# Placing the last two experts' rows for three of five tiles, and gathering the stored rows for the other two

## The chip, the cores and the metric

The kernel runs on one core of a Trainium2 chip. The metric is the device time of one execution in microseconds (us); the time of a kernel is the median over its runs. One further execution was recorded by the hardware profiler: its span is the time from the first to the last instruction. Engines: PE (TensorE) multiplies matrices, DVE (VectorE) and ACT (ScalarE) work on tiles of 128 partitions, POOL (GpSimd) issues the indirect DMAs, SP (SyncE) issues most other DMAs.

## What is computed

One layer of a diffusion trunk with a linear-attention mixer, then a mixture of experts. 640 tokens (128 of context, 512 latent) pass through. The end of it is what matters here: each token takes the weighted outputs of two of 16 gated experts, adds them to its residual row, and the sum is normalised.

```python
# hier_moe: combine holds the two weights of each token's two picks
up = jnp.einsum('td,edf->tef', hf, p['moe_w1'])
gate = jnp.einsum('td,edf->tef', hf, p['moe_w3'])
act = jax.nn.silu(gate) * up * combine[:, :, None]
return jnp.einsum('tef,efd->td', act, p['moe_w2']).reshape(B, T, D)
...
x = x + (ga2 * hier_moe(h2, p)).astype(x.dtype)
...
y_prompt = rmsnorm(x, final_g)
```

## The kernel before

The 640 tokens are five tiles (NT = 5) of 128 rows by 1024 columns; tile 0 is the context. Each engine has its own instruction list, and the lists meet in semaphores; the order of each list is the order in which its code is written. PSUM is eight banks that a list of jobs (`jobs`) takes in turn.

**Experts.** Experts run in rounds; round r serves the slots r*128 to r*128 + 127 of every expert, and later rounds are entered only if some expert has more than 128 tokens. In a round, POOL gathers the tokens of each expert's 128 slots (`gather_rows`, L941), PE turns them, multiplies by the up and gate weights (job "ug"), DVE and ACT form the gated activations (L2002 to L2007; ACT's exponential and copies, all at L966), PE turns those (job "aT") and multiplies by the down weights (jobs "dn", two halves of 512 columns). DVE multiplies each half by a gain (weight times gate) on the way out of PSUM into `yo`, which has one buffer for even and one for odd experts (`rows_of`, L1995). The gain itself is made in two steps: ACT scales one row (`gain_b`), DVE adds the other part (L1990).

**How rows come back to tokens.** For experts 0 to 13 (LE = 14) ACT stores `yo` in DRAM (`rows_out`, L1310, tensor `expert_rows_dram`), 512 KB an expert. When these stores have landed, POOL issues ten indirect DMAs, two a tile: the first adds the row of each token's first pick into the residual `x1[:, t]` (L955), the second puts the row of the second pick in `second_rows[t]` (L958). A pick of expert 14 or 15 finds a row of zeros, written near the start (L679). Rows of experts 14 and 15 are never stored: PE places them, multiplying a 0/1 matrix (`own_slot`) by `yo`, two products for each half of each tile (jobs "sel").

**The end.** After expert 15's rows, DVE does for each tile: add `second_rows[t]` (L2020), add the two PSUM halves of the placed rows (L2024), and, one tile behind, the final scaling by the root of the mean square and the final gain (`final_rows`, L1954) into `acc`. ACT makes the root in between (a squaring pass with sum, a logarithm, an exponential), and SP stores each finished tile (L798).

Of the kernel before, what the change touches and what calls it, by code (L numbers as in the profile page):

```python
# [5 lines left out]
def trunk_program(nc, x_prompt, x_sample, state_rwkv, state_gla, c, c_ctx, norm1_g, norm2_g, w_ada, b_ada,  # L6
# [37 lines left out]
    LE = NE - 2  # L44
    CH = 64
# [13 lines left out]
    with ctx:  # L59
# [225 lines left out]
        ys_dram = nc.dram_tensor("expert_rows_dram", (NE * P, D), f32, kind="Internal").ap()  # L285
# [95 lines left out]
        for r in range(NT):  # L381
# [14 lines left out]
            jobs += [("sel", r, t, h) for t in range(NT) for h in range(2)]  # L396
# [187 lines left out]
        s_finr = sem("final_rstd")  # L584
        s_yout = sem("y_out")
# [66 lines left out]
        def _(sp):  # L652
# [15 lines left out]
            for i in range(RING, NS1):  # L668
# [4 lines left out]
                if i == 3 * RING:  # L673
# [15 lines left out]
            def inverse_back(h):  # L689
# [3 lines left out]
                if h == 0:  # L693
                    sp.wait_ge(s_zd, 48)
# [88 lines left out]
            def load_experts(r, count_known):  # L783
# [12 lines left out]
                for t in range(NT):  # L796
                    sp.wait_ge(s_yout, r * NT + t + 1)
                    sp.dma_start(y_prompt[0] if t == 0 else y_sample[0, (t - 1) * P:t * P, :], acc[:, t]).then_inc(s_ydma, 16)  # L798
# [6 lines left out]
        def _(pool):  # L805
# [127 lines left out]
            def gather_rows(r, count_known):  # L933
# [28 lines left out]
        def _(act):  # L962
# [42 lines left out]
            act.wait_ge(s_zd, 48)  # L1005
# [300 lines left out]
            def expert_copies(r, count_known):  # L1306
# [5 lines left out]
                act.wait_ge(s_ga2, 16)  # L1312
                for e in range(NE):
                    i = r * NE + e
                    if e == 0:
# [11 lines left out]
                    if i >= 2:  # L1327
                        act.wait_ge(s_yrow, i - 1)
                    if e == 0:
                        wait_result(act, "sw", r)  # L1330
                    tell(A(gain_b[e % 2], ga2b[:, 1], scale=slot_w[:, e:e + 1]), s_gain)
# [4 lines left out]
                for t in range(NT):  # L1336
                    wait_result(act, "sel", r, t, 1)
                    if r >= 1:
                        act.wait_ge(s_yout, (r - 1) * NT + t + 1)
# [7 lines left out]
        def _(dve):  # L1347
# [599 lines left out]
            def final_rows(r, t):  # L1947

                dve.wait_ge(s_finr, r * NT + t + 1)
                if r == 0 and t == 0:  # L1950
                    dve.wait_ge(s_fg, 16)
# [4 lines left out]
            def expert_gates(r, count_known):  # L1956
# [18 lines left out]
                own(STT(R["ib"], R["ps"], float(-(r + LE) * P), R["in"], ALU.add, ALU.mult))  # L1975
                own(TS(R["ib"], R["ib"], float(LE * P), None, ALU.add))
# [7 lines left out]

                def rows_of(e):
                    i = r * NE + e
                    at = r * (LE // 2) + e // 2
                    gain = gain_b[e % 2]
                    dve.wait_ge(s_gain, i + 1)
                    own(STT(gain, ga2b[:, 0], slot_w[:, NE + e:NE + e + 1], gain, ALU.mult, ALU.add))  # L1990
# [23 lines left out]
                rows_of(NE - 1)  # L2014
                if r == 0:
                    count_known()

                def rows_complete(t):
                    dve.wait_ge(s_yg[t], 32 * (r + 1))
                    own(TT(x1[:, t], x1[:, t], second_rows[t], ALU.add))  # L2020
# [12 lines left out]
        def _(pe):  # L2033
# [665 lines left out]
            def expert_products(r, count_known):  # L2699
# [57 lines left out]
                for t in range(NT):  # L2757
# [37 lines left out]
```

## Time and profile before

| | us |
|---|---|
| median of 3 runs | 942.36 |
| the three runs | 940.07, 942.71, 942.36 |
| the profiled execution | 939.88 |
| its span | 937.0 |

The profiled execution lies below the median of the runs; durations and waits are read from it. Over the whole span PE is busy 849.1 us (91%), DVE 566.8, ACT 331.2, POOL 155.2. The clock granted to PE is full in the stretch of the change until its last product; the mean over the span is 0.973. A line of the timeline gives start and duration in us, engine, source line, operation, output and inputs, shape, how often it stands in a row, and in brackets how long the engine was idle before it and what ended that. POOL's DMA lines show the time POOL spends to issue; "DMA to landing" is from the start of the issue to the last byte.

### The profile page before, as it was taken

The numbers are of one execution on the slowest core, as the hardware profiler recorded it, in microseconds if no ns is written. First come the engines' busy times: TensorE is split into PE (matmuls) and PEld (weight loads), VectorE is DVE, ScalarE is ACT, GpSimd is POOL, SyncE is SP. The second block draws the span as 40 slices with busy tenths as digits, with TensorE's granted clock in tenths as the row PEclk, the third lists the DMA queues.
The fourth block names the chain that finished last, engine by engine and source line by source line (L and its number), as shares of the span: only waits on it lengthen the run. The fifth ranks groups of instructions, "written<-read, shape, count | busy, mean of one in ns | idle before, by whom it ended". The sixth has DMA issues, their size and how long they took to land.

```text
span 937.0 us, 21506 instructions
## 1 busy us (share of the span) xinstructions
PE 849.1 (91%) x8890; PEld 518.2 (55%) x8890; DVE 566.8 (60%) x942; ACT 331.2 (35%) x582; POOL 155.2 (17%) x301
## 2 busy tenths in 40 slices
PE   2899999999999988988888888899994999999995
PEld 0455455566455454677777777745563544444542
DVE  2424036789988789666555565688356344444467
ACT  3221111142034467375667664312211222222213
POOL 7000111112000103424232231010002000000051
PEclk9999999999999999999999999999995999999998
DMA  9911323222255201111212222591064899999956
GB/s 332 382 39 65 130 91 101 91 84 80 86 179 180 91 0 27 36 24 32 44 33 37 42 43 54 186 351 77 26 222 132 287 358 370 362 365 372 311 142 220
DMA packets 120815, 142.44 MB, mean 152 GB/s; under 512 B 49996, under 2 KB 86280, under 8 KB 120328
## 3 DMA queue, kind: packets, MB, share of 16 engines
q1 hardware_dynamic: 111880, 116.55, 37.9%
q0 software_dynamic: 3744, 13.63, 4.7%
q10 hardware_dynamic: 5088, 10.82, 3.0%
q8 instruction: 73, 1.20, 0.5%
q14 instruction: 30, 0.25, 0.1%
HBM read 122.99 MB, written 18.00 MB: 150 GB/s over the span
## 4 chain that ended last, share of the span: by engine, by line
PE 79%; DVE 9%; DMA 4%; issue 3%; ACT 3%; SPq 0%; ACTq 0%; DVEq 0%; POOLq 0%
PE bank L2035 72%; PE bank L2039 7%; DMA region<-in_w_ada_dram 3%; DVE rk_r L1449 1%; ACT region L966 1%; DMA region<-in_w_in_dram 1%; DVE region L1449 1%; ACT ada_row_buffers L966 1%; DVE rk_r L1450 1%; DVE cl_b L1954 1%; DVE region L2024 1%; DMA rk_r<-h_rows_dram,slot_tokens 0%; DVE region L2020 0%; ACT w_sb L966 0%; DVE region L2003 0%
## 5 line engine op out<-in xcount | busy, mean ns | idle before, releaser
L2035 PE MATMUL bank<-region 64*64 64x64 f32 (+3 forms) x3900 | 399.2, 297 | 15.7 <-issue 6.1
L2035 PEld LDWEIGHTS bank<-region 64*64 64x64 f32 (+1 forms) x3900 | 231.2, 147 | 169.9 <-issue 158.8
L966 ACT ACTIVATE region<-bank 128x256 f32<-128x256 f32 (+3 forms) x215 | 97.2, 452 | 345.6 <-PE bank L2035 259.1
L2035 PE MATMUL bank<-region,rk_r 128*128 128x512 f32 x176 | 79.9, 608 | 0.8 <-issue 0.8
L2039 PE MATMUL bank<-ident,region 128*128 128x128 f32 (+2 forms) x403 | 61.7, 282 | 12.8 <-DMA region<-in_c_dram 10.9
L2039 PEld LDWEIGHTS bank<-ident,region 128*128 128x128 f32 (+2 forms) x403 | 44.1, 142 | 30.9 <-issue 23.5
L2002 DVE TENSOR_SCALAR region<-region 128x256 f32<-128x256 f32 x16 | 4.7, 295 | 93.3 <-ACT region L966 93.3
L1449 DVE SCALAR_TENSOR_TENSOR rk_r<-region,vec,rk_r 128x512 f32<-128x512 f32 x64 | 50.1, 783 | 11.1 <-ACT rk_r L966 9.0
L2035 PEld LDWEIGHTS bank<-region,rk_r 128*128 128x128 f32 x176 | 33.5, 196 | 39.5 <-issue 38.3
L941 POOL DMA_INDIRECT rk_r<-h_rows_dram,slot_tokens x16 | 16.0, 999 | 225.6 <-PE bank L2039 127.2
L1631 DVE TENSOR_TENSOR region<-bank,region 128x256 f32<-128x256 f32 x60 | 25.5, 424 | 39.2 <-PE bank L2035 37.9
L2035 PE MATMUL bank<-scratch,region 64*64 64x64 f32 (+1 forms) x688 | 41.7, 228 | 6.1 <-issue 3.2
L2035 PE MATMUL bank<-vtok_b,region 64*64 64x64 f32 x928 | 44.4, 222 | 1.6 <-DVE region L1660 1.6
L2035 PE MATMUL bank<-region,scratch 64*64 64x128 f32 (+1 forms) x512 | 35.8, 410 | 9.6 <-DMA region<-in_w_ada_dram 8.8
L2035 PEld LDWEIGHTS bank<-scratch,region 64*64 64x64 f32 (+1 forms) x688 | 39.1, 140 | 7.2 <-issue 7.2
L2035 PEld LDWEIGHTS bank<-vtok_b,region 64*64 64x64 f32 x928 | 41.3, 138 | 2.8 <-DVE region L1631 1.7
L966 ACT ACTIVATE region<-region 128x256 f32<-128x256 f32 (+1 forms) x27 | 24.7, 915 | 43.5 <-DVE region L1466 42.8
L966 ACT ACTIVATE ada_row_buffers<-bank 128x512 f32<-128x512 f32 x29 | 17.3, 597 | 55.0 <-PE bank L2039 51.0
L2035 PE MATMUL bank<-cl_b,ada_row_buffers 128*128 128x512 f32 x80 | 35.8, 596 | 0.1
L2035 PE MATMUL bank<-rk_r,ada_row_buffers 128*128 128x512 f32 x80 | 35.6, 593 | 0.0
L2035 PE MATMUL bank<-cl_b,rk_r 128*128 128x512 f32 x80 | 35.2, 593 | 0.0
L873 POOL TENSOR_TENSOR region<-kk_b,region 128x512 f32<-128x512 f32 x10 | 13.0, 1300 | 133.4 <-PE bank L2039 105.7
(283 smaller groups left out, 1137.2 us busy)
## 6 DMA issues: line engine op xcount, KB each, us to landing
region<-in_moe_w_dram SPq DMA_DIRECT2D x38, 1024.0 KB, 10.0
region<-in_w_ada_dram SPq DMA_DIRECT2D x12, 2048.0 KB, 8.8
region<-in_w_in_dram SPq DMA_DIRECT2D x6, 2048.0 KB, 9.1
cl_b<-in_moe_w_dram SPq DMA_DIRECT2D x10, 1024.0 KB, 11.1
expert_rows_dram<-yg_b ACTq DMA_DIRECT2D x14, 512.0 KB, 6.8
region<-late_condition_dram SPq DMA_DIRECT2D x3, 1024.0 KB, 9.4
a_rows_dram<-region SPq DMA_DIRECT2D x20, 128.0 KB, 2.5
region<-inverse_rows_dram SPq DMA_DIRECT2D x20, 128.0 KB, 3.0
```

The lines of the kernel that those rows point to most:

```text
L873: tell(pool.tensor_tensor(g.b, kkT[:, :, tok], aa[:, d, :, tok], ALU.mult), s_t1)
L941: pool.indirect_dma_start(out=xg[:, i % 3], out_offset=None, in_=h2_dram, in_offset=bass.IndirectOffsetOnAxis(ap=idx[:, e:e + 1], axis=0)) ...
L966: return act.activation(out, in_, func, **kw)
L1449: own(STT(out, lat[:, i:i + GH, j:j + GW], tap(c_, i, j), out, ALU.mult, ALU.add))
L1450: own(STT(dst[:, 0:P], line[:, 1:P + 1], tap(c_, 1, 1), dst[:, 0:P], ALU.mult, ALU.add))
L1631: out_of(TT(dst[:, hp::2], bank((n, h, hp))[:, 0:RC * HD].rearrange("p (h i) -> p h i", h=RC), src[:, hp::2], ALU.add), n, h, hp)
L1954: tell(STT(acc[:, t], x1[:, t], rstd[:, t:t + 1], fg, ALU.mult, ALU.mult), s_yout)
L2002: own(TS(sg[:, s], sg[:, s], 1.0, None, ALU.add))
L2024: out_of(TT(v, v, bank(("sel", r, t, h))[:, :], ALU.add), "sel", r, t, h)
L2035: return pe.matmul(out, lhsT, rhs, start=start, stop=stop)
L2039: return pe.transpose(out, in_, ident[0:n, 0:n])
```

## The change

PE places the last two experts' rows for tiles 0, 1 and 2 only (`PLACED = 3`). ACT stores the rows of experts 14 and 15 as well, and POOL waits for all sixteen stores before it gathers for tiles 3 and 4, whose picks of experts 14 and 15 now point at the stored rows. In the placed tiles such picks point at one added row of zeros (row NE*P), for which DVE makes one more small step and SP one more store near the start. The gain steps of experts 14 and 15 are moved ahead of expert 15's gate arithmetic on ACT and DVE. At the end DVE's list is rewritten: tile 0's add of gathered rows stands before expert 15's multiplies, those of tiles 1 and 2 before the placed rows are added, and the tiles are finished in the order 0, 1, 3, 2, 4 (`ROWS_ORDER`), on ACT and SP too.

```diff
+    PLACED = 3
+    ROWS_ORDER = (0, 1, 3, 2, 4)
...
-        ys_dram = nc.dram_tensor("expert_rows_dram", (NE * P, D), f32, kind="Internal").ap()
+        ys_dram = nc.dram_tensor("expert_rows_dram", (NE * P + 1, D), f32, kind="Internal").ap()
...
-            jobs += [("sel", r, t, h) for t in range(NT) for h in range(2)]
+            jobs += [("sel", r, t, h) for t in range(PLACED) for h in range(2)]
...
+                    sp.dma_start(ys_dram[NE * P:NE * P + 1, :].rearrange("a (b n) -> (a b) n", n=512), cl_b[0:2, 0:512]).then_inc(s_zd, 16)
...
                 for q in range(2):
-                    pool.wait_ge(s_ys[q], 16 * (r + 1) * (LE // 2))
-                pool.wait_ge(s_zd, 48)
+                    pool.wait_ge(s_ys[q], 16 * (r * (NE // 2) + LE // 2))
+                pool.wait_ge(s_zd, 64)
...
                 for t in range(NT):
+                    if t == PLACED:
+                        for q in range(2):
+                            pool.wait_ge(s_ys[q], 16 * (r + 1) * (NE // 2))
...
                 for e in range(NE):
                     i = r * NE + e
+                    if e == NE - 1:
+                        slot_gain(e)
...
-                    if 0 < e <= LE:
+                    if e < NE - 1:
+                        slot_gain(e)
+                    if e > 0:
                         rows_out(e - 1)
+                rows_out(NE - 1)
...
-                own(STT(R["ib"], R["ps"], float(-(r + LE) * P), R["in"], ALU.add, ALU.mult))
-                own(TS(R["ib"], R["ib"], float(LE * P), None, ALU.add))
+                own(STT(R["ib"], R["ps"], float(-(r + NE) * P), R["in"], ALU.add, ALU.mult))
+                placed = by_pick(R["ib"])[:, :, 0:PLACED]
+                own(STT(placed, placed, float((LE - NE) * P), placed, ALU.is_lt, ALU.mult))
+                own(TS(R["ib"], R["ib"], float(NE * P), None, ALU.add))
...
+                    if e == NE - 1:
+                        gain_of(LE)
+                        gain_of(NE - 1)
...
-                rows_complete(0)
-                for t in range(1, NT):
-                    rows_complete(t)
-                    final_rows(r, t - 1)
-                final_rows(r, NT - 1)
+                gathered(0)
+                rows_of(NE - 1)
+                if r == 0:
+                    count_known()
+                gathered(1)
+                gathered(2)
+                placed_rows(0)
+                placed_rows(1)
+                final_rows(r, 0)
+                gathered(3)
+                final_rows(r, 1)
+                placed_rows(2)
+                gathered(4)
+                final_rows(r, 3)
+                final_rows(r, 2)
+                final_rows(r, 4)
```

How the lists of DVE and POOL change in order. On DVE, from expert 15's gates to the end of the first two tiles, before (`yg_b` is `yo`, `region0` holds `second_rows`, `region3` is `x1`, `cl_b` is `acc`, L1990 the gain, L1995 the multiply):

```order
L2007 TENSOR_TENSOR region1<-bank4,region1 128x256
L1990 SCALAR_TENSOR_TENSOR region1<-region1,scratch 128x1024
L1995 TENSOR_TENSOR yg_b<-bank5,region1 128x512
L1995 TENSOR_TENSOR yg_b<-bank6,region1 128x512
L1996 MEMSET small 128x1
L1990 SCALAR_TENSOR_TENSOR kk_b<-region1,scratch,kk_b 128x1024
L1995 TENSOR_TENSOR yg_b<-bank0,kk_b 128x512
L1995 TENSOR_TENSOR yg_b<-bank1,kk_b 128x512
L1996 MEMSET small 128x1
L2020 TENSOR_TENSOR region3<-region3,region0 128x1024
L2024 TENSOR_TENSOR region3<-region3,bank2 128x512
```

And now (L2009 the gain, L2021 the multiply, L2045 the add of gathered rows, L2052 the add of placed rows):

```order
L2036 TENSOR_TENSOR region1<-bank4,region1 128x256
L2021 TENSOR_TENSOR yg_b<-bank5,region1 128x512
L2021 TENSOR_TENSOR yg_b<-bank6,region1 128x512
L2022 MEMSET small 128x1
L2045 TENSOR_TENSOR region3<-region3,region0 128x1024
L2021 TENSOR_TENSOR yg_b<-bank0,kk_b 128x512
L2021 TENSOR_TENSOR yg_b<-bank1,kk_b 128x512
L2022 MEMSET small 128x1
L2045 TENSOR_TENSOR region3<-region3,region0 128x1024 x2
L2052 TENSOR_TENSOR region3<-region3,bank2 128x512
```

The two gain steps are gone from behind the gates, and the adds of gathered rows of tiles 0, 1 and 2 stand ahead of the first placed rows.

On POOL, the gathers of expert rows of tiles 2, 3 and 4, before:

```order
L955 DMA region<-expert_rows_dram,pick_slots 128x1024
L958 DMA region<-expert_rows_dram,pick_slots 128x1024
L955 DMA region<-expert_rows_dram,pick_slots 128x1024
L958 DMA region<-expert_rows_dram,pick_slots 128x1024
L955 DMA region<-expert_rows_dram,pick_slots 128x1024 [waits filled]
```

And now:

```order
L962 DMA region<-expert_rows_dram,pick_slots 128x1024
L965 DMA region<-expert_rows_dram,pick_slots 128x1024
L962 DMA region<-expert_rows_dram,pick_slots 128x1024 [waits expert_rows_stored1,expert_rows_stored0]
L965 DMA region<-expert_rows_dram,pick_slots 128x1024
L962 DMA region<-expert_rows_dram,pick_slots 128x1024 [waits filled]
```

The order is the same; the seventh gather, tile 3's first, has a wait for the stores of both kinds of experts.

## Rows read from the trace of the kernel before

**Rows 1.** Timeline of PE: down products of expert 15, then all placing products.

```profile
905.41 3.70 PE L2035 MATMUL bank<-region 128*128 128x512 f32 x8 [0.53 <-ACT region L966]
909.58 17.41 PE L2035 MATMUL bank<-yg_b,vtok_b 128*128 128x512 f32 x40 [0.47 <-DVE yg_b L1995]
```

**Rows 2.** Timeline of DVE from expert 14's gain step to the last scaling.

```profile
904.42 1.28 DVE L1990 SCALAR_TENSOR_TENSOR region<-region,scratch 128x1024 f32<-128x1024 f32 x1
...
908.64 1.42 DVE L1995 TENSOR_TENSOR yg_b<-bank,kk_b 128x512 f32<-128x512 f32 x2
...
911.14 1.23 DVE L2020 TENSOR_TENSOR region<-region 128x1024 f32<-128x1024 f32 x1 [0.96 <-DVE small L1996]
...
916.79 0.69 DVE L2024 TENSOR_TENSOR region<-region,bank 128x512 f32<-128x512 f32 x1 [0.77 <-PE bank L2035]
...
918.84 1.23 DVE L2020 TENSOR_TENSOR region<-region 128x1024 f32<-128x1024 f32 x1
920.10 1.41 DVE L2024 TENSOR_TENSOR region<-region,bank 128x512 f32<-128x512 f32 x2
921.54 1.28 DVE L1954 SCALAR_TENSOR_TENSOR cl_b<-region,small,kk_b 128x1024 f32<-128x1024 f32 x1
922.86 1.23 DVE L2020 TENSOR_TENSOR region<-region 128x1024 f32<-128x1024 f32 x1
...
931.46 1.28 DVE L1954 SCALAR_TENSOR_TENSOR cl_b<-region,small,kk_b 128x1024 f32<-128x1024 f32 x1 [0.58 <-ACT small L966]
```

**Rows 3.** Timeline of POOL: gathers of expert rows (tiles 0, 0, 1, 2, 4).

```profile
899.40 1.57 POOL L955 DMA_INDIRECT region<-expert_rows_dram,pick_slots  x1 [42.03 <-DMA expert_rows_dram<-yg_b]
901.28 0.98 POOL L958 DMA_INDIRECT region<-expert_rows_dram,pick_slots  x1 [0.30 <-issue]
...
904.41 0.98 POOL L958 DMA_INDIRECT region<-expert_rows_dram,pick_slots  x1 [0.31 <-issue]
...
907.55 1.91 POOL L958 DMA_INDIRECT region<-expert_rows_dram,pick_slots  x1 [0.30 <-issue]
...
915.37 0.97 POOL L958 DMA_INDIRECT region<-expert_rows_dram,pick_slots  x1 [0.30 <-issue]
```

**Rows 4.** Line L958, one gather at a time: landing, tiles 0, 1, 2, 4.

```profile
DMA to landing us min/median/max: 6.4/6.4/6.4
...
DMA to landing us min/median/max: 7.4/7.4/7.4
...
DMA to landing us min/median/max: 8.1/8.1/8.1
...
DMA to landing us min/median/max: 8.2/8.2/8.2
```

**Rows 5.** DMA queues from 902 to 916 us: packets, MB, share of 16 engines.

```profile
q0 software_dynamic: 931, 3.42, 101.5%
```

**Rows 6.** Waits from 895 us to the end: total, times, longest us.

```profile
DVE region L2002 <- ACT region L966: 5.5, 1, 5.5
```

**Rows 7.** Busy time by stage (PE, PEld, DVE, ACT, POOL, PEclk, DMA share, GB/s).

```profile
897.00:898.00 1.00, 1.00 (x4) 0.41 (x3) 0.00 (x0) 0.00 (x0) 0.00 (x0) 1.00 0.99 406
```

**Rows 8.** Single stores: expert 13's rows, expert 12's, first output, last output.

```profile
L1310 ACTq DMA_DIRECT2D expert_rows_dram<-yg_b x1: 326/326/326, 896.0 to 896.0; - x1
DMA to landing us min/median/max: 2.6/2.6/2.6
...
DMA to landing us min/median/max: 4.7/4.7/4.7
...
DMA to landing us min/median/max: 5.6/5.6/5.6
...
DMA to landing us min/median/max: 3.8/3.8/3.8
```

**Rows 9.** Timeline of DVE: expert 0's gates, after the pick slots.

```profile
730.95 0.29 DVE L2002 TENSOR_SCALAR region<-region 128x256 f32<-128x256 f32 x1 [8.57 <-ACT region L966]
```

**Rows 10.** The page's DMA issues: KB each, median us to landing.

```profile
region<-in_moe_w_dram SPq DMA_DIRECT2D x38, 1024.0 KB, 10.0
...
region<-late_condition_dram SPq DMA_DIRECT2D x3, 1024.0 KB, 9.4
```

More of the change, by code:

```diff
@@ L584, in trunk_program @@
         s_finr = sem("final_rstd")
+        s_late = sem("late_tile_rows_complete")
         s_yout = sem("y_out")
@@ L693, in inverse_back @@
                 if h == 0:
-                    sp.wait_ge(s_zd, 48)
+                    sp.wait_ge(s_zd, 64)
                 if p >= 1:
@@ L795, in load_experts @@
                     count_known()
-                for t in range(NT):
-                    sp.wait_ge(s_yout, r * NT + t + 1)
+                for n, t in enumerate(ROWS_ORDER):
+                    sp.wait_ge(s_yout, r * NT + n + 1)
                     sp.dma_start(y_prompt[0] if t == 0 else y_sample[0, (t - 1) * P:t * P, :], acc[:, t]).then_inc(s_ydma, 16)
@@ L1312, in expert_copies, with slot_gain @@
                 act.wait_ge(s_ga2, 16)
+                def slot_gain(e):
+                    i = r * NE + e
+                    if i >= 2:
+                        act.wait_ge(s_yrow, i - 1)
+                    if e == 0:
+                        wait_result(act, "sw", r)
+                    tell(A(gain_b[e % 2], ga2b[:, 1], scale=slot_w[:, e:e + 1]), s_gain)
                 for e in range(NE):
                     i = r * NE + e
+                    if e == NE - 1:
+                        slot_gain(e)
                     if e == 0:
@@ L1326, in expert_copies @@
                     copy_out(aT[:, i % 2], ("aT", i), bank(("aT", i))[:, 0:FT * P].rearrange("p (f t) -> p f t", f=FT))
[L1327 to L1331, printed above, removed]
-                    if 0 < e <= LE:
+                    if e < NE - 1:
+                        slot_gain(e)
+                    if e > 0:
                         rows_out(e - 1)
+                rows_out(NE - 1)
                 if r == 0:
                     count_known()
-                for t in range(NT):
-                    wait_result(act, "sel", r, t, 1)
+                for n, t in enumerate(ROWS_ORDER):
+                    if t < PLACED:
+                        wait_result(act, "sel", r, t, 1)
+                    else:
+                        act.wait_ge(s_late, r * (NT - PLACED) + t - PLACED + 1)
                     if r >= 1:
-                        act.wait_ge(s_yout, (r - 1) * NT + t + 1)
+                        act.wait_ge(s_yout, (r - 1) * NT + n + 1)
                     own(A(junk, x1[:, t], ACT.Square, accum_out=rstd[:, t:t + 1]))
@@ L1947, in final_rows @@
             def final_rows(r, t):
-                dve.wait_ge(s_finr, r * NT + t + 1)
-                if r == 0 and t == 0:
+                n = ROWS_ORDER.index(t)
+                dve.wait_ge(s_finr, r * NT + n + 1)
+                if r == 0 and n == 0:
                     dve.wait_ge(s_fg, 16)
@@ L1983, in expert_gates, with gain_of @@
                     own(ins) if e < NE - 1 else tell(ins, s_own)
+                def gain_of(e):
+                    gain = gain_b[e % 2]
+                    dve.wait_ge(s_gain, r * NE + e + 1)
+                    own(STT(gain, ga2b[:, 0], slot_w[:, NE + e:NE + e + 1], gain, ALU.mult, ALU.add))
                 def rows_of(e):
                     i = r * NE + e
-                    at = r * (LE // 2) + e // 2
+                    at = r * (NE // 2) + e // 2
                     gain = gain_b[e % 2]
-                    dve.wait_ge(s_gain, i + 1)
-                    own(STT(gain, ga2b[:, 0], slot_w[:, NE + e:NE + e + 1], gain, ALU.mult, ALU.add))
+                    if e < LE:
+                        gain_of(e)
                     if at:
@@ L2012, in expert_gates, with gathered, placed_rows @@
                         rows_of(e - 1)
[L2014 to L2018, printed above, removed]
+                def gathered(t):
                     dve.wait_ge(s_yg[t], 32 * (r + 1))
-                    own(TT(x1[:, t], x1[:, t], second_rows[t], ALU.add))
+                    ins = TT(x1[:, t], x1[:, t], second_rows[t], ALU.add)
+                    own(ins) if t < PLACED else tell(ins, s_late)
+                def placed_rows(t):
                     for h in range(2):
@@ L2756, in expert_products @@
                 pe.wait_ge(s_own, r + 1)
-                for t in range(NT):
+                for t in range(PLACED):
                     for h in range(2):
```

2 lines of the change are left out of this document (1 added, 1 removed).

## The prediction

> **What bounds the kernel now.** The change touches only the last 37 us, so the question is what binds there, and the page's shares, which PE leads, can't tell. I read the timelines of PE and DVE for that stretch. PE finishes the down products of expert 15 and starts the placing products at 909.58; all forty of them take 17.41 us, 3.48 us a tile [rows 1]. DVE waits for PE only twice among the tiles, the second time at 916.79 for 0.77 us; from there it is never idle until the last tile, where it waits 0.58 us for ACT's root [rows 2]. A tile costs DVE 1.26 us for the add of the gathered rows (918.84 to 920.10), 1.44 for the two adds out of PSUM (to 921.54) and 1.32 for the final scaling: 4.02 us against PE's 3.48. The tail is DVE's. The last scaling starts at 931.46.
>
> The third view is POOL's timeline with the landing times. The ten gathers are issued from 899.40 to 915.37 and hold nothing up, because DVE asks for them late: those of tile 0 are in at 901.28 + 6.4 = 907.7, those of tile 2 at 907.55 + 8.1 = 915.65, those of tile 4 at 915.37 + 8.2 = 923.6, while the adds that use the first and the last begin at 911.14 and, two tiles after 918.84, at 926.9 [rows 2 to 4]. They are slow and they fill the DMA engines: from 902 to 916 the software queue moved 3.42 MB and took 101.5% of all sixteen [rows 5], 0.245 MB a us. So there is some slack between gather and use, 3.3 us at tile 4, and none in the DMA engines.
>
> **What is removed.** Sixteen of the forty placing products: 7.0 us of PE after 920 by 17.41/40 each, worth nothing to the end, since DVE was behind PE there. Four DVE adds out of PSUM, 2 x 1.44 = 2.9 us [rows 2]: these were on the path. The gain step of expert 15 (1.28 us, as long as a final scaling [rows 2]) moves ahead of the gate arithmetic, into the time in which DVE and ACT wait for the up product (DVE was idle 5.5 us there [rows 6]); the gain of expert 14 goes with it. Both were on the path between the gates and the placing products.
>
> **What takes their place on DVE.** Before, after expert 15's gates, gain, multiply, gain, multiply ran from 904.42 to 910.06 [rows 2]. Now the first multiply runs from 904.42 to 905.9. Then comes tile 0's add of gathered rows, ahead of expert 15's multiply, and its rows land at 907.7. It ends at 907.7 + 1.26 = 908.96. Expert 15's two multiplies are 0.72 each: 909.68 and 910.40, PE having its products ready by 909.1 (905.41 + 3.70 [rows 1]). So the gain step's 1.3 us are eaten by this wait, and expert 15's rows are ready 0.3 us later than before (908.64 + 1.42 [rows 2]). With the marker and the issue (0.15 us in before) ACT stores them at about **910.6**. Next is tile 1's add (landed 911.8 in before, perhaps 913 now), then tile 2's.
>
> Tile 2's rows: in before they landed at 915.65. By then 3.42 MB and the little before 902 had moved, of which 3.15 MB are tiles 0 to 2; the rest, some 0.4 MB or 1.6 us at 0.245 MB a us, was tile 3's and is gone from this place. Two stores of 0.52 MB come in, 1.3 us each at the 0.406 MB a us of the store of expert 13, which had the engines alone [rows 7]. Together 915.65 - 1.6 + 2.6 = 916.7. From the end of tile 2's add, 917.9, DVE has 2 x 1.44 + 1.32 = 4.2 us of work (tiles 0 and 1 placed, tile 0 scaled), then what is left needs tile 3's gathers: free at **922.1**.
>
> **The wait that is added.** POOL may issue tile 3's and tile 4's gathers only when the store of expert 15's rows has landed. Behind that wait stand four gathers on POOL; behind them stand DVE's adds of tiles 3 and 4, ACT's roots and the last three scalings. The price is the landing of a store issued at 910.6 into full DMA engines. The rows bound it: 2.6 us for expert 13's, alone; 4.7 for expert 12's, with weight loads going on; 5.6 for the first output, issued at 918.8 with tile 4's gathers in flight [rows 8]. The last is the nearest, since here too about six microseconds of gathers are queued, and I take it: 916.2. POOL started 0.8 us after the landing in before (896.0 + 2.6 = 898.6 to 899.40 [rows 3, 8]), so **917.0**.
>
> From there I copy the pattern of tiles 0 and 1, the other pairs that started into idle engines: issue 899.40, landed at +8.3 (907.7) and +12.4 (904.41 + 7.4 = 911.8) [rows 3, 4]. Tile 3's rows are in at **925.3** and tile 4's at **929.4**.
>
> DVE: tile 3's add 925.3 to 926.56, tile 1's scaling to 927.9, tile 2 placed to 929.3, tile 4's add from 929.4 to 930.66, scalings of tiles 3 and 2 to 933.3. ACT's root takes 1.28 + 0.58 = 1.9 us from the end of an add (in before the last scaling waited for it 0.58 us after the one ahead, which had begun when the add ended [rows 2]): 932.6 for tile 4, hidden. The last scaling starts at 933.3 against 931.46: **1.8 us later**. Its store goes out over the same idle engines (3.8 us then [rows 8]); it follows the one before it by 1.3 us, one transfer, so nothing is added.
>
> **Small terms.** One more DVE step on 128x6 in the pick slots, at most as much as a full scaling on 1024 columns did (1.28), with 8.57 us of idle time behind it [rows 9]: nothing. One 4 KB store and a count of 64 for 48 near 39 us, waited for much later: nothing. Picks of experts 14 and 15 in the placed tiles now all read one zero row instead of many. The nearest rows for reads of one address are the broadcast loads: 9.4 us for 1 MB against 10.0 for weights of the same size [rows 10]. So no loss is booked, and a gain is not either.
>
> The sum: 939.88 (profiled execution: span 937.0 and 2.88 around it) + 1.8 = 941.7. That execution lies 2.5 below the median of the three runs, 942.36, so against the median it is 942.36 + 1.8 = **944.2**.
>
> **A rule against the rows.** The second gathers of tiles 0, 1, 2 and 4 landed 6.4 to 8.2 us after their issue [rows 4], and a pair took about 4 us (907.7, 911.8, 915.65). "DMA: Bandwidth & Descriptors" of the Trainium skill (Anatomy of one DMA) gives a transfer from GpSimd about 2.0 us plus its bytes by 436 GB/s, which is an estimate of 3.2 us for half a megabyte. Tile 0's, into nearly idle engines, already took twice that. What it would make of the end is the third rival.
>
> **Rivals.** They all hang on when tile 4's gathers land. The end is unchanged when tile 4's add starts at 931.46 - 1.26 - 2 x 1.32 = 927.6, that is with POOL at 915.2 and the store landed 3.8 us after its issue.
> (1) The store gets through quickly, 2.6 us: POOL at 914.0, tile 3 in at 922.3, tile 4 at 926.4. DVE then binds: 922.3 and 1.26, 1.32, 1.44 make 926.3, and 926.4 and 1.26, 1.32, 1.32 make 930.3 for the last scaling, 1.2 us early: 941.2. For it: stores alone do that. Against: the engines are full at 910.6.
> (2) Slower: the gathers hold the store back until they are through (7 us or more: landed 917.6, POOL 918.4), and the outputs of tiles 0 and 1, 1.3 us of the engines each, now lie among tile 4's gathers. Tile 4 in at 930.8 to 932.1, the end 3.2 to 4.6 us late: 945.6 to 947.0. It counts as slower from a landing of 6.6 us on. For it: the 5.6 us row already reached past the end of tile 4's gathers (924.4 against 923.6). Against: weights and stores shared the engines in 4.7.
> (3) The gathers land in about 3.8 us, as a lone output store does; the engines' fullness would be a matter of how their time is counted. POOL at 914.0, tile 3 in at 919.7, tile 4 at 922.8, DVE binds throughout, from placed tile 1 (PE, 916.8) on: the last scaling near 927.6, 3.9 us early: 938.5. The Trainium skill's formula leads here. The landings of [rows 4] speak against it.
> That the change leaves work where it was is excluded: DVE's and PE's instruction lists show the steps gone.
>
> **Chances.** Forecast, 0.3 to 2.8 us later: 0.50. (1), 1.2 us early to 0.3 late: 0.22. (2): 0.22. (3): 0.06. A measurement here tells about 0.3%, 2.8 us, from no change. So faster 0.06, same 0.72, slower 0.22. The range leaves out (3) and the far end of (2) with the scatter of a median (0.07 to 2.3 us between the runs shown): 940.6 to 947.0. The likeliest case's own is 942.7 to 945.2.
>
> **What would show it.** In the profile of the changed kernel: DVE waits before the first add of gathered rows, to about 907.7; the last store of expert rows is issued near 910.6 and lands in 5 to 6 us; POOL has one gap of 6 to 7 us before the seventh gather, which starts near 917; PE ends 10 us after its first placing product; DVE waits for a DMA three times (tiles 2, 3 and briefly 4), and its last three scalings stand close together. If POOL starts again before 915.2, or DVE does not wait at tile 4, the forecast is wrong toward (1); if the gap of POOL ends after 918, toward (2). If tile 3's rows take much under 8.3 us from that start, my copy of the first pairs' pattern is the step that failed.

## The result and the profile after

The changed kernel takes 947.72 us (median of 14 runs, 941.51 to 952.73), the kernel before 941.35 (14 runs, 939.45 to 946.63). The ratio is 1.0063, with a 95% interval of 1.0042 to 1.0083: slower, by 5.9 us of 941. The forecast was 1.8 us slower, 944.2 us, called no change because 1.8 us is less than the 2.8 us that a measurement can tell; its range went up to 947.0.

The profiled execution took 950.49 us, its span is 948.7. Part of its distance to the kernel before is scatter between executions: expert 15's exponential on ACT, before which the two kernels do the same work, starts at 907.49 instead of 900.90. So I measure from that exponential in every trace ("after" is the changed kernel). To the end of the span it is 937.0 - 900.90 = 36.1 us in before and 948.7 - 907.49 = **41.2** in after, and the last scaling starts after 30.6 and 36.0 us. These 5.1 and 5.4 us are near the 5.9 of the runs, but the two are not the same quantity. The part of the device time that lies outside the span is 2.88 us in the profiled execution of before and only 1.8 in the changed kernel (1.70 to 1.84 in all 14 runs), so the span grew by about 1.1 us more than the time did. When both kernels ran again, the medians rose by 5.3 us in time and by 6.3 in span, and the stretch from the exponential by 6.2. What shortens the part outside the span is open; it also reads about 1.8 us in every other variant below but gain_moved and plain_gathers.

The timeline of DVE in after, from expert 14's multiply to the end (columns as in [rows 2]):

```profile
911.01 1.42 DVE L2021 TENSOR_TENSOR yg_b<-bank,region 128x512 f32<-128x512 f32 x2
...
914.47 1.23 DVE L2045 TENSOR_TENSOR region<-region 128x1024 f32<-128x1024 f32 x1 [1.92 <-DMA region<-expert_rows_dram,pick_slots]
915.73 1.42 DVE L2021 TENSOR_TENSOR yg_b<-bank,kk_b 128x512 f32<-128x512 f32 x2
...
919.79 1.23 DVE L2045 TENSOR_TENSOR region<-region 128x1024 f32<-128x1024 f32 x1 [2.52 <-DMA region<-expert_rows_dram,pick_slots]
925.04 1.28 DVE L2045 TENSOR_TENSOR region<-region 128x1024 f32<-128x1024 f32 x1 [4.02 <-DMA region<-expert_rows_dram,pick_slots]
926.36 2.85 DVE L2052 TENSOR_TENSOR region<-region,bank 128x512 f32<-128x512 f32 x4
929.60 1.28 DVE L1973 SCALAR_TENSOR_TENSOR cl_b<-region,small,kk_b 128x1024 f32<-128x1024 f32 x1 [0.39 <-ACT small L973]
934.14 1.22 DVE L2045 TENSOR_TENSOR region<-region 128x1024 f32<-128x1024 f32 x1 [3.25 <-DMA region<-expert_rows_dram,pick_slots]
935.40 1.28 DVE L1973 SCALAR_TENSOR_TENSOR cl_b<-region,small,kk_b 128x1024 f32<-128x1024 f32 x1
936.72 1.41 DVE L2052 TENSOR_TENSOR region<-region,bank 128x512 f32<-128x512 f32 x2
939.61 1.22 DVE L2045 TENSOR_TENSOR region<-region 128x1024 f32<-128x1024 f32 x1 [1.49 <-DMA region<-expert_rows_dram,pick_slots]
940.87 3.93 DVE L1973 SCALAR_TENSOR_TENSOR cl_b<-region,small,kk_b 128x1024 f32<-128x1024 f32 x3
```

Where [rows 2] had one wait of 0.77 us for PE and one of 0.58 for ACT, every add of gathered rows (L2045) now waits for its DMA: 1.92, 2.52, 4.02, 3.25 and 1.49 us, 13.2 in all. The steps that were taken off DVE are gone, and DVE now waits for the gathers longer than they were worth. What the gathers wait for stands in POOL's timeline of after (tile 2's second gather, then tiles 3 and 4; compare [rows 3], where nothing but 0.30 us stands between two gathers):

```profile
914.09 0.98 POOL L965 DMA_INDIRECT region<-expert_rows_dram,pick_slots  x1 [0.30 <-issue]
925.07 1.55 POOL L962 DMA_INDIRECT region<-expert_rows_dram,pick_slots  x1 [10.00 <-DMA expert_rows_dram<-yg_b]
926.92 0.97 POOL L965 DMA_INDIRECT region<-expert_rows_dram,pick_slots  x1 [0.30 <-issue]
928.20 1.55 POOL L962 DMA_INDIRECT region<-expert_rows_dram,pick_slots  x1 [0.30 <-issue]
930.05 1.68 POOL L965 DMA_INDIRECT region<-expert_rows_dram,pick_slots  x1 [0.30 <-issue]
```

Ten microseconds of POOL's idle time end with the store of expert 15's rows. The chain that ended last in after, in order of time (start, us, what), goes through that store and then through the tenth gather:

```profile
916.46 0.69 DVE yg_b L2021
...
917.31 7.03 DMA expert_rows_dram<-yg_b
...
925.07 1.19 POOL region L962
...
930.05 9.46 DMA region<-expert_rows_dram,pick_slots
...
939.61 1.24 DVE region L2045
```

It has no placing product in it, where the chain of before had its longest piece of the last 33 us:

```profile
909.58 7.12 PE bank L2035 x16
```

The store takes 7.0 us where [rows 8] gave 5.6 for the nearest, the tenth gather 9.5 where [rows 4] had at most 8.2. Between them the DMA engines run dry, which they did not do in before while gathers were left. Busy time by stage in after (columns as in [rows 7]; the last but one is the DMA share):

```profile
918.00:924.00 6.00, 6.00 (x15) 2.66 (x14) 1.23 (x1) 0.00 (x0) 0.00 (x0) 1.00 1.04 328
924.00:930.00 6.00, 3.21 (x8) 1.14 (x6) 4.43 (x6) 2.10 (x5) 4.07 (x3) 1.00 0.48 76
930.00:940.00 10.00, 0.00 (x0) 0.00 (x0) 5.15 (x6) 4.48 (x12) 1.68 (x1) 0.53 0.92 275
```

From 924 to 930 the engines are 48% busy: 3 us of gather time lost, while four of the ten gathers have still to be done. PE's clock falls to half (0.53) after 930, but PE has nothing left to do there.

### The profile page after: what moved, and what is told of

It reads as the page before. It is cut to its first block, busy times and chain, and to the rows that moved or that the text cites. A ratio compares the mean times of both kernels' runs of the same rounds, so it can differ in the third digit from the quotient of the medians.

```text
span 948.7 us, 21466 instructions
## 1 busy us (share of the span) xinstructions
PE 847.2 (89%) x8874; PEld 517.5 (55%) x8874; DVE 564.5 (60%) x939; ACT 331.2 (35%) x582; POOL 154.2 (16%) x301
## 4 chain that ended last, share of the span: by engine, by line
PE 78%; DVE 8%; DMA 6%; issue 4%; ACT 2%; SPq 0%; POOL 0%; POOLq 0%; ACTq 0%; DVEq 0%
PE bank L2074 71%; PE bank L2078 7%; DMA region<-in_w_ada_dram 3%; DVE rk_r L1467 1%; ACT region L973 1%; DMA region<-expert_rows_dram,pick_slots 1%; DMA region<-in_w_in_dram 1%; DMA expert_rows_dram<-yg_b 1%; DVE region L1467 1%; DVE rk_r L1468 1%; ACT ada_row_buffers L973 1%; DMA rk_r<-h_rows_dram,slot_tokens 0%; ACT w_sb L973 0%; DVE cl_b L1973 0%; DVE region L2032 0%
## 5 line engine op out<-in xcount | busy, mean ns | idle before, releaser
L945 POOL DMA_INDIRECT rk_r<-h_rows_dram,slot_tokens x16 | 16.1, 1007 | 225.6 <-PE bank L2078 127.4
L2074 PE MATMUL bank<-region,scratch 64*64 64x128 f32 (+1 forms) x512 | 36.6, 419 | 9.6 <-DMA region<-in_w_ada_dram 8.8
L2074 PE MATMUL bank<-cl_b,ada_row_buffers 128*128 128x512 f32 x80 | 35.8, 596 | 0.1
```

The costliest lines, as they stand in the source:

```text
L945: pool.indirect_dma_start(out=xg[:, i % 3], out_offset=None, in_=h2_dram, in_offset=bass.IndirectOffsetOnAxis(ap=idx[:, e:e + 1], axis=0)) ...
L2074: return pe.matmul(out, lhsT, rhs, start=start, stop=stop)
```

## Experiments

Three variants leave something out of the result (no_wait, no_stores and plain_gathers, as their texts say), so their ratios price a part and are not those of a usable kernel. For each run the table gives, from expert 15's exponential, the start of the last scaling and the end of the span; from the first gather's issue, the landing of tile 2's second gather, POOL's resumption with the seventh gather and the landing of the tenth; and the time as a ratio to the kernel before with its 95% interval. The trace has no landing time for tile 2's second gather in plain_gathers.

| kernel | last scaling | end | tile 2 in | seventh issued | tenth in | ratio |
|---|---|---|---|---|---|---|
| before | 30.6 | 36.1 | 16.2 | 10.4 | 24.2 | 1 |
| after | 36.0 | 41.2 | 19.0 | 19.1 | 33.6 | 1.0063 (1.0042 to 1.0083) |
| again | 36.9 | 42.3 | 19.6 | 20.1 | 34.5 | 1.0053 (1.0031 to 1.0074) |
| before_again | 30.6 | 36.1 | 16.6 | 10.4 | 24.8 | 1.0007 (0.9978 to 1.0036) |
| no_wait | 31.3 | 36.6 | 19.1 | 9.4 | 28.4 | 1.0009 (0.9985 to 1.0033) |
| no_stores | 28.7 | 33.9 | 16.5 | 9.4 | 24.9 | 0.9981 (0.9958 to 1.0005) |
| spread_zeros | 36.8 | 42.0 | 19.5 | 20.5 | 34.4 | 1.0062 (1.0036 to 1.0088) |
| tile2_behind | 36.6 | 41.8 | 24.3 | 19.0 | 32.1 | 1.0058 (1.0024 to 1.0093) |
| outputs_held | 34.9 | 40.2 | 20.2 | 19.1 | 32.4 | 1.0049 (1.0024 to 1.0075) |
| gain_moved | 29.8 | 35.1 | 16.5 | 9.4 | 25.8 | 1.0000 (0.9976 to 1.0024) |
| all_placed | 31.3 | 36.8 | 16.2 | 9.4 | 23.7 | 0.9981 (0.9958 to 1.0004) |
| pool_adds | 30.6 | 35.8 | 16.4 | 9.4 | 25.3 | 0.9996 (0.9971 to 1.0022) |
| pe_adds | 31.1 | 36.8 | 16.3 | 9.5 | 24.8 | 1.0021 (0.9994 to 1.0047) |
| plain_gathers | 30.6 | 35.9 | | 7.5 | 17.7 | 0.9984 (0.9963 to 1.0006) |

(tile2_behind resumes at 15.8 with tile 2's gathers, the fifth; its seventh follows at 19.0.)

**Both kernels again, unchanged.**

> The changed kernel once more, unchanged. All theories: the stretch from the start of ACT's exponential for expert 15 to the end of the span (36.1 us in the kernel before: 937.0 - 900.90; 41.2 in the changed one: 948.7 - 907.49) repeats within 1 us, whatever the execution's whole time is. If it does not, the 5.1 us difference is scatter and not the change.

> The kernel before once more, unchanged. All theories: the stretch from expert 15's exponential to the end repeats within 1 us of 36.1, the last scaling starts 30 to 31 us after the exponential (30.6), and the ten gathers are in 24 to 26 us after the first one's issue (24.2).

Measured: the kernel before repeats to a tenth of a microsecond in both columns. The changed one comes out 1.1 us longer, 42.3, just over the microsecond allowed, so a difference of about a microsecond between two variants of it says little, and 5 to 6 us between the kernels is real.

**The wait, and the traffic.** In no_wait POOL's wait is gone and the two stores go to rows that nobody reads:

```diff
-                    if t == PLACED:
-                        for q in range(2):
-                            pool.wait_ge(s_ys[q], 16 * (r + 1) * (NE // 2))
...
-                placed = by_pick(R["ib"])[:, :, 0:PLACED]
+                placed = by_pick(R["ib"])
...
-                    act.dma_start(ys_dram[e * P:(e + 1) * P, :], yo[:, e % 2]).then_inc(s_ys[e % 2], 16)
+                    row = e * P if e < LE else (e + 2) * P + 1
+                    act.dma_start(ys_dram[row:row + P, :], yo[:, e % 2]).then_inc(s_ys[e % 2], 16)
```

In no_stores they are not made at all:

```diff
-                    if e > 0:
+                    if 0 < e <= LE:
                         rows_out(e - 1)
-                rows_out(NE - 1)
```

> Leaves out the last two experts' rows for tiles 3 and 4: they are stored, but in other rows, and the picks point at the zero row, so POOL needs no wait before the seventh gather. Theory W (POOL's wait for the store is what costs): the ten gathers go out in a row, tile 3's rows are in before DVE is free, and the stretch from expert 15's exponential to the end falls from 41.2 to 35 to 36 us. Theory C (the two stores and the gathers take each other's DMA time, the wait is minor): it stays above 39.

> Leaves out the last two experts' rows for tiles 3 and 4, and their two stores too; no wait on POOL. What it gains over no_wait is the price of the two stores as traffic. Theory W: 1 to 2 us (2.6 us of transfer, part of it hidden), stretch 33.5 to 35 us, tile 2's rows in about 2.6 us sooner after the first gather than in the changed kernel. Theory C: 4 us or more.

Measured: without the wait the end comes 36.6 us after the exponential, 4.6 less than in after (5.7 less than in again); the expectation said 35 to 36. Without the stores it is 33.9, 2.7 less again, over the 1 to 2 expected and under the 4 of the other theory. So the wait is the larger part and the traffic the smaller, and the traffic is hardly hidden. The waits of no_wait in its last 39 us (total, times, longest) show where it lands, and the same line of no_stores follows:

```profile
DVE region L2047 <- DMA region<-expert_rows_dram,pick_slots: 8.5, 3, 4.1
```

```profile
DVE region L2041 <- DMA region<-expert_rows_dram,pick_slots: 5.9, 3, 2.6
```

Three waits instead of five, the longest for tile 2's rows, which come at 19.1 us against 16.5 without the stores. That is two transfers of 1.3 us, in full. And they come at 19.1 with tile 3's gathers queued behind them, against 19.0 to 20.2 in the four executions in which these are held back (after, again, spread_zeros, outputs_held): removing them from behind tile 2 gave nothing back. The last three scalings follow without a gap.

The three rows compose the result: the work taken from DVE, in its new order, is worth 30.6 - 28.7 = 1.9 us, the stores cost 31.3 - 28.7 = 2.6, the wait 36.0 - 31.3 = 4.7 (5.6 by again). Even with stores and wait for nothing, the change would have gained only 1.9 us. One reason stands in the second line: without stores and without POOL's wait DVE still waits 5.9 us for gathers, because the new order asks for the rows of tiles 0, 1 and 2 before any placed row is added. No run has the old order of tiles 1 and 2 with three placed tiles, so what that order costs is open.

**One row of zeros, or many.**

```diff
-                own(STT(placed, placed, float((LE - NE) * P), placed, ALU.is_lt, ALU.mult))
+                moved = by_pick(R["in"])[:, :, 0:PLACED]
+                own(TS(moved, placed, float((LE - NE) * P), float(2 * P), ALU.is_ge, ALU.mult))
+                own(TT(placed, placed, moved, ALU.add))
```

> The changed kernel, but picks of experts 14 and 15 in the placed tiles read 256 rows of zeros, each slot its own, instead of one row; complete result. Theory W: no change, stretch 41 us, tile 2's rows in 19.1 us after the first gather's issue as in the changed kernel (925.04 - 905.94). Theory Z (one row read by many partitions slows the gathers, and this holds the store back): tile 2's rows in 2 us or more sooner, and the stretch 2 us or more shorter.

Measured: tile 2 in at 19.5, end 42.0, both between those of the two executions of the changed kernel (19.0 and 19.6, 41.2 and 42.3). The shared row is not the cause.

**Why the store takes so long.** POOL's wait is moved two gathers forward:

```diff
-                    if t == PLACED:
+                    if t == PLACED - 1:
```

> The changed kernel with POOL's wait two gathers earlier: tile 2's pair too goes out only after the store of expert 15's rows. Complete result. Theory Q (that store is slow because it shares the DMA engines with the gathers queued ahead of it): with four gathers in front, in 13.8 us after the first one's issue, the store (issued 11.4 us after it) lands in 3 to 4.5 us and POOL resumes 15 to 16.5 us after its first gather, not 19.1 to 20.5. Theory F (a store there takes 7 to 8 us whatever is queued): POOL resumes at 19 or later. The whole is not shorter by either, since six gathers follow instead of four.

Measured: expert 15's store lands 3.7 us after its issue, and POOL resumes at 15.8, as theory Q said. One store of one size, issued at the same point of the program, 11.3 to 11.5 us after the first gather: 3.7 us with four gathers issued before it, 7.0, 8.0, 8.3 and 6.9 with six (after, again, spread_zeros, outputs_held), 10.9 with seven before it and three more while it was under way (no_wait). Its landing line in tile2_behind, in after and in no_wait:

```profile
DMA to landing us min/median/max: 3.7/3.7/3.7
```

```profile
DMA to landing us min/median/max: 7.0/7.0/7.0
```

```profile
DMA to landing us min/median/max: 10.9/10.9/10.9
```

These landings go with the last gather issued before the store. That one is in at 13.9 us in tile2_behind and the store at 15.1; in after 19.0 and 18.4, in again 19.6 and 19.3, in spread_zeros 19.5 and 19.7, in outputs_held 20.2 and 18.4. In no_wait it is the seventh, in at 21.8, and the store at 22.4, six microseconds ahead of the tenth gather, which was issued after it. So the store came in from 1.8 us before to 1.2 us after that gather. Expert 14's store was in the same queue ahead of it in all six (in 14.1 to 15.0 us after the first gather's issue), so it is not what differs between them. tile2_behind gives one thing more. Its six last gathers had the engines to themselves (the first output was ready only when they were nearly in) and took 32.1 - 15.8 = 16.3 us from issue to landing; the first six of before took 16.2. The first four of them took 28.3 - 15.8 = 12.5 us, the 12.4 of the pattern that the prediction copied. That pattern is sound where nothing else moves.

**The outputs among the last gathers.**

```diff
+                sp.wait_ge(s_yg[NT - 1], 32 * (r + 1))
                 for n, t in enumerate(ROWS_ORDER):
```

> The changed kernel, but SP stores the first finished tile only when tile 4's gathers have landed, so that no output shares the engines with tiles 3 and 4. Complete result. Theory O (the outputs of tiles 0 and 1 are what stretched the last four gathers, from the 12.4 us of the pattern to 14.5): from the seventh gather's issue to the landing of the tenth 12.4 to 13 us, DVE's last scaling starts 1.5 to 2 us sooner after expert 15's exponential than in the changed kernel (36.0 us). If it stays at 14 or more, another reason stretches them.

Measured: from the seventh gather to the tenth's landing 13.3 us (32.4 - 19.1), just above the 12.4 to 13 of theory O, against 14.5 (after), 14.4 (again) and 13.9 (spread_zeros); the last scaling starts at 34.9, 1.1 us sooner than in after and 2.0 than in again. That points to the outputs of tiles 0 and 1 as the cause of 0.6 to 1.2 us of the stretch over 12.4; the difference is no larger than the scatter between executions of the changed kernel, so it is likely and not shown. The 0.9 us that are left have no experiment of their own; the four gathers of tile2_behind did not have them.

**The parts of the change that are not the late gathers.** In gain_moved the kernel before has only the gain steps moved:

```diff
+                    if e == NE - 1:
+                        gain_of(LE)
+                        gain_of(NE - 1)
                     dve.wait_ge(s_sg, i + 1)
...
-                    own(STT(gain, ga2b[:, 0], slot_w[:, NE + e:NE + e + 1], gain, ALU.mult, ALU.add))
+                    if e < LE:
+                        gain_of(e)
```

all_placed is the changed kernel without its late gathers and without their wait and stores: it keeps the gain steps and tile 0's early add, places five tiles and ends them in the old order:

```diff
-    PLACED = 3
-    ROWS_ORDER = (0, 1, 3, 2, 4)
+    PLACED = 5
+    ROWS_ORDER = (0, 1, 2, 3, 4)
...
+                for t in range(1, NT):
+                    gathered(t)
+                    placed_rows(t)
+                    final_rows(r, t - 1)
+                final_rows(r, NT - 1)
```

> The kernel before with one part of the change alone: the gain steps of experts 14 and 15 ahead of expert 15's gates. Complete result. Theory P (PE's down products of expert 15 end at 909.1, so the placing products can't start before): placing starts 8.2 us after expert 15's exponential instead of 8.7, and the stretch to the end falls from 36.1 to 35.6 to 35.9 us. Theory G (the gain steps were on the path, as the prediction had it): it falls by 1.3 us or more.

> The change without late gathers: gain steps moved, tile 0's add of gathered rows ahead of expert 15's multiply, but all five tiles placed by PE, no store of the last two experts' rows, no wait on POOL; the tiles end in the old order. Complete result. Theory W: the last scaling starts 29.8 to 30.6 us after expert 15's exponential (29.8 in gain_moved, since DVE again waits 2 us for tile 0's gathers), so the rewritten order by itself neither costs nor gains 1 us, and the kernel's time is that of the kernel before within 0.3%. If it is 32 us or more, the order of DVE and not the late gathers holds a good part of the loss.

Measured: gain_moved starts the last scaling at 29.8, 0.7 us sooner, and ends at 35.1, 1.0 us sooner: more than theory P gave and less than theory G. Its time is that of before within 0.24%. PE and DVE in gain_moved:

```profile
908.66 3.70 PE L2049 MATMUL bank<-region 128*128 128x512 f32 x8 [0.53 <-issue]
912.20 17.33 PE L2049 MATMUL bank<-yg_b,vtok_b 128*128 128x512 f32 x40
```

```profile
910.78 0.69 DVE L2006 TENSOR_TENSOR yg_b<-bank,kk_b 128x512 f32<-128x512 f32 x1 [1.57 <-PE bank L2049]
912.47 0.69 DVE L2006 TENSOR_TENSOR yg_b<-bank,kk_b 128x512 f32<-128x512 f32 x1 [1.00 <-PE bank L2049]
```

With the gains out of the way DVE waits 1.57 and 1.00 us for the down products, 2.6 us, all that the two gain steps had taken. But for 0.6 us they stood beside PE's work and not on the path: placing starts 8.05 us after the exponential instead of 8.68. In all_placed, tile 0's add waits 2.13 us for its gathers ahead of expert 15's multiply, and PE begins placing only at 9.4 us; the last scaling is at 31.3, where 29.8 to 30.6 was expected: 1.4 us later than gain_moved, as is the start of placing. So that early add costs more than it saves here. The changed kernel has it too, ahead of the store of expert 15's rows that POOL waits for; no run takes it out there. It is under the 32 us at which the order would have been a main cause.

**Could a version beat both?** Since DVE sets the end of the kernel before, two variants on top of gain_moved hand an add to another engine.

```diff
+                for t in range(3, NT):
+                    pool.wait_ge(s_yg[t], 32 * (r + 1))
+                    tell(pool.tensor_tensor(x1[:, t], x1[:, t], second_rows[t], ALU.add), s_late)
```

> The kernel before with the gain steps moved and with POOL, idle after its tenth gather, adding the gathered rows of tiles 3 and 4 in DVE's place. Complete result. If DVE's cadence sets the tail of the kernel before (4.02 us a tile against PE's 3.48), taking 2 x 1.26 us from it brings the last scaling 1.5 to 2.3 us sooner (PE's last product is then the bound): stretch 33.8 to 34.6 us. If POOL's adds take much over 3 us each or slow DVE, the gain is under 1 us.

Measured: no gain (last scaling at 30.6 against 29.8). Tile 4's rows land 25.3 us after the first gather, and POOL's add of them takes 3.32 us, so DVE waits for POOL; tile 3's add by POOL also held a DVE scaling up:

```profile
922.06 2.35 POOL L963 TENSOR_TENSOR region<-region 128x1024 f32<-128x1024 f32 x1 [3.89 <-DMA region<-expert_rows_dram,pick_slots]
927.14 3.32 POOL L963 TENSOR_TENSOR region<-region 128x1024 f32<-128x1024 f32 x1 [2.72 <-DMA region<-expert_rows_dram,pick_slots]
```

```profile
923.24 2.26 DVE L1964 SCALAR_TENSOR_TENSOR cl_b<-region,small,kk_b 128x1024 f32<-128x1024 f32 x1
...
930.55 1.41 DVE L2045 TENSOR_TENSOR region<-region,bank 128x512 f32<-128x512 f32 x2 [2.29 <-POOL region L963]
```

```diff
+                        if t == 2:
+                            ins = mm(b[:, :], ident[:, :], second_rows[t][:, h * 512:(h + 1) * 512], start=False, stop=True)
```

> gain_moved, and PE adds tile 2's second gathered rows into the PSUM bank of its placed rows by one more product with the identity for each half (2 x 0.43 us), so that DVE skips that tile's add of 1.26 us. Complete result. With DVE's cadence as the bound after tile 1, the last scaling starts 0.8 to 1.2 us sooner than in gain_moved (29.8 us after expert 15's exponential); if PE has become the bound, under 0.5.

Measured: 31.1, worse than gain_moved by 1.3. The timeline of PE (the added product of tile 2's second half) and then of DVE's two adds of tile 2's placed rows:

```profile
922.67 1.02 PE L2050 MATMUL bank<-region,ident 128*128 128x512 f32 x2
```

```profile
921.26 0.69 DVE L2039 TENSOR_TENSOR region<-region,bank 128x512 f32<-128x512 f32 x1 [0.73 <-PE bank L2050]
923.80 0.69 DVE L2039 TENSOR_TENSOR region<-region,bank 128x512 f32<-128x512 f32 x1 [1.86 <-PE bank L2050]
```

The trace counts two MATMULs of about 0.43 us for each product of the code, so PE got 4 x 0.43 = 1.7 us more to do, twice what the expectation had. The 1.23 us saved on DVE came back as 2.6 us of waiting for PE: at tile 2 DVE was only just behind PE. No version was measurably faster than the kernel before.

**What the accumulating gathers cost.**

```diff
                                             in_offset=bass.IndirectOffsetOnAxis(ap=pos[:, t:t + 1], axis=0),
-                                            compute_op=ALU.add).then_inc(s_yg[t], 16)
```

> The kernel before with the first gather of each tile as a plain one: it overwrites the residual row instead of adding to it, so the residual is left out of the result. Theory A (the accumulating half makes the gathers slow, since it reads its target too): a pair takes 2.6 to 3.3 us of the engines instead of 3.9, and the ten are in 17 to 20 us after the first one's issue instead of 24.2. Theory R (every gather by rows is slow): 23 us or more.

Measured: the ten are in after 17.7 us instead of 24.2, 1.3 us less a tile, and the last scaling stays at 30.6. The software queue from 902 to 914 us of that run, which moved 4.37 MB in 12 us, 0.36 MB a us against 0.245 in [rows 5]:

```profile
q0 software_dynamic: 1195, 4.37, 96.4%
```

In the kernel before this is no gain, because its tail does not hang on the gathers. In the changed one, whose tail does, it should be one; that was not run.

## Why the prediction was wrong

The mechanism was the right one, named in the prediction as the added wait. The forecast failed on two terms of that wait that were too small: the landing of expert 15's store (5.6 us, measured 7.0 and 8.0) and tile 4's landing after POOL's restart (12.4 us, measured 14.5 and 14.4). In microseconds from expert 15's exponential:

| step | predicted | after | again |
|---|---|---|---|
| expert 15's rows ready | 9.5 | 9.7 | 9.6 |
| tile 2's rows in | 15.8 | 17.5 | 18.1 |
| store of expert 15's rows, landing time | 5.6 | 7.0 | 8.0 |
| POOL issues tile 3's first gather | 16.1 | 17.6 | 18.5 |
| tile 4's rows in | 28.5 | 32.1 | 33.0 |
| last scaling starts | 32.4 | 36.0 | 36.9 |

- **What bounds the kernel, and what the removed work is worth.** Right for the tail (DVE), and before_again repeats it. The four adds were called worth 2.9 us on the path; no_stores, where they are gone and nothing is late by the wait, gains 1.9, with the gain steps' part and DVE's 5.9 us of waits for gathers in it.
- **The gain steps** were said to be on the path. Mostly wrong: gain_moved gains 0.7 us of 2.6, because DVE then waits for PE's down products. The prediction used PE's 909.1 two sentences later without drawing this. It did not hurt the sum, which had the gain eaten by tile 0's wait.
- **The wait at tile 0** and the readiness of expert 15's rows: right within 0.2 us.
- **Tile 2's rows** were 1.7 us later than predicted (17.5 for 15.8). The step that failed is "the rest, some 0.4 MB or 1.6 us, was tile 3's and is gone from this place": tile 2 is in at 19.0 to 20.2 us with tile 3 held back and at 19.1 with it queued. The two stores' 2.6 us were right, and stood alone. This did not enter the sum, since DVE had to wait for tile 3's rows anyway.
- **The store's landing** is the first term of the sum that failed: 1.5 us too small in after, 2.4 in again. It was carried over from the first output as a duration of 5.6 us, "since here too about six microseconds of gathers are queued". The rows don't say that: the output went out at 918.8 with gathers until 923.6, 4.8 us, while the store at 910.6 had, by the prediction's own figure for tile 2 (916.7), 6.1 us of them ahead. What carries over is the order: the output came in 0.8 us after the last gather issued before it (924.4 against 923.6). That gives 917.5 here, a landing of 6.9 us, and POOL at 918.3, which is 17.4 us after the exponential; 17.6 was measured. tile2_behind and no_wait show that this landing is set by the gathers issued before it (3.7, 6.9 to 8.3 and 10.9 us for four, six and seven). POOL's gap ended at 17.6 us, 918.5 on the clock of before, past the 918 that the prediction gave as the sign for rival (2).
- **Tile 4 at 12.4 us from POOL's restart** was 14.5, the second term of the sum that failed, by 2.1 us. The pattern itself holds (12.5 for the first four gathers after the restart in tile2_behind), but the outputs of tiles 0 and 1 lay among these four gathers. Rival (2) had this term at up to 1.3 us, the sum did not; outputs_held returns 1.2, little more than the scatter. Some 0.9 us stay unexplained.
- **The part outside the span** was kept at 2.88 us; it is 1.8 in every run of the changed kernel. This 1.1 us went the other way and hid part of the miss.
- **From tile 4's landing to the last scaling**: 3.9 predicted, 3.9 measured.

1.5 and 2.1 us are the two mis-sized terms, and 1.8 + 1.5 + 2.1 = 5.4 is what after shows. Rival (2), with a chance of 0.22, was the case that came. Its landing of 7 us was right for after; its price, 3.2 to 4.6 us, was still 0.8 too low, because it allowed the outputs 1.3 us where the stretch was 2.1. The likeliest case should have had both of the things that rival (2) had: the store behind the gathers, as the output's row showed, and the outputs among the last ones.

The Trainium skill's formula for a transfer from GpSimd ("DMA: Bandwidth & Descriptors", Anatomy of one DMA: about 2.0 us plus bytes by 436 GB/s, an estimate of 3.2 us here) is not borne out by any gather read in these runs; a plain one in plain_gathers, with others queued, took 6.1. Rival (3) falls with it. The same page (Queues, rings and completion order) says that each DMA engine goes round between the queues that have work for it. The trace of after agrees: expert 14's store was issued at 912.63, 0.4 us after the fifth gather, and landed 8.3 us later at 920.9, 2.1 us ahead of that gather (912.24 + 10.8).

## What to carry to other kernels

A transfer that leaves the path of the engines can land on the path of the DMA engines: before adding a store and a dependent load near the end, write down the queue at that moment and price the store by when the transfers issued before it are in, the restart by the time in which the DMA engines run dry, and the rest by whatever else will be sent by then. A step that stands between two others on the engine that sets the end is not on the path if the next one would wait for another engine anyway; look for that wait's end before counting the step as gain. And take no credit for transfers queued behind the one that is waited for: here they were worth nothing.

## What the runs showed of the hardware

- A gather of 128 rows of 4 KB that adds into its target costs the DMA engines more than a plain one: ten gathers, five of them adding, took 24.2 us, and with all ten plain 17.7, and the queue moved 0.36 MB a us instead of 0.245.
- The landing of a 0.5 MB store from ACT's queue grew with the gathers issued before it on GpSimd's: 2.6 us with none [rows 8], then 3.7 with four, 6.9 to 8.3 with six, and 10.9 with seven and three more that followed it.
- GpSimd's add of 128x1024 took 2.35 and 3.32 us where DVE's takes 1.23, and a DVE step with two operands in SBUF that met the first one took 2.26 instead of 1.28. The Trainium skill states such a block ("SBUF — State Buffer", SBUF: two separate sides: of a DVE instruction with two inputs in SBUF and a GpSimd one that reads SBUF, the one that starts first gets the shared ports for its whole length and the other waits), and the trace agrees: POOL's add ended at 924.41 and the DVE step 1.1 us after it. The second add, begun at 927.14 beside a DVE scaling that ended at 928.26, ended 2.2 us after that.
